# Second norm of a transformer layer: token block 0 normed first, the normed x gathered, gate-up waits by halves, turned h copied first

## The reference

```python
x = layer_norm(DN_ALPHA * x + mixed, ln1_g[l], ln1_b[l])
x = layer_norm(DN_ALPHA * x + memory_cross_attention(x, mem, w_cq[l], w_ckv[l], w_co[l]), ln2_g[l], ln2_b[l])
x = layer_norm(DN_ALPHA * x + moe_ffn(x, w_router[l], router_bias[l], w_exp_gu[l],
                                      w_exp_down[l], w_sh_gu[l], w_sh_down[l]), ln3_g[l], ln3_b[l])
...
scores = jax.nn.sigmoid(jnp.dot(t, w_router).astype(jnp.float32))
choice = scores + router_bias.astype(jnp.float32)
...
gates = jnp.zeros((n_tok, N_EXPERTS), jnp.float32).at[jnp.arange(n_tok)[:, None], idx].set(w).astype(t.dtype)
y = (jax.nn.silu(gu[:, :SHARED_FF]) * gu[:, SHARED_FF:]) @ w_sh_down
for e in range(N_EXPERTS):
    gu = t @ w_exp_gu[e]
    h = jax.nn.silu(gu[:, :EXPERT_FF]) * gu[:, EXPERT_FF:]
    y = y + gates[:, e:e + 1] * (h @ w_exp_down[e])
```

## Time and profile before

| | us |
|---|---|
| median of three runs | 1021.77 (1020.12 to 1022.16) |
| the profiled execution | 1021.97 |
| its span | 1019.80 |
| TensorE busy | 993.3 (97%) |
| VectorE busy | 524.5 (51%) |
| ACT busy | 376.4 (37%) |
| GpSimd busy | 56.3 (6%) |

### The profile page before, as it was taken

How to read it: one execution, slowest core, us unless ns; L and a number is a source line. 1 busy time by engine, 2 the same in 40 slices (tenths; PEclk the granted TensorE clock), 3 DMA queues, 4 the chain that set the end, 5 groups by cost and what they waited for, 6 DMA issues and landing times.

```text
span 1019.8 us, 15454 instructions
## 1 busy us (share of the span) xinstructions
PE 993.3 (97%) x6370; PEld 711.6 (70%) x6371; DVE 524.5 (51%) x1049; ACT 376.4 (37%) x687; POOL 56.3 (6%) x53
## 2 busy tenths in 40 slices
PE   8999999999999999999999999999999999999994
PEld 7998999999999999998974444444444444444432
DVE  6899455675769966855677222322223222222223
ACT  5665435556577744455321211121112111211112
POOL 0000202324200000000010000000000000000000
PEclk9999999999999999999999999999999999999998
DMA  8564534333344555658837999999999999999972
GB/s 305 188 226 146 185 123 167 124 125 125 125 166 166 181 192 182 233 207 350 347 141 280 419 419 421 420 419 420 420 418 420 420 420 420 421 420 419 420 326 83
DMA packets 41653, 290.85 MB, mean 285 GB/s; under 512 B 4712, under 2 KB 5872, under 8 KB 6896
## 3 DMA queue, kind: packets, MB, share of 16 engines
q1 hardware_dynamic: 40800, 284.62, 70.6%
q0 software_dynamic: 784, 5.24, 1.3%
HBM read 288.78 MB, written 1.06 MB: 284 GB/s over the span
## 4 chain that ended last, share of the span: by engine, by line
PE 86%; DVE 10%; issue 2%; DMA 1%; ACT 1%; SPq 0%; ACTq 0%; DVEq 0%
PE stream L1548 24%; PE stream L1876 22%; PE stream L1900 11%; PE stream L1573 8%; PE work L1865 6%; DVE w_lo L972 3%; DVE acc L1008 3%; PE stream L1824 2%; PE stream L1828 1%; PE stream L1826 1%; PE stream L1830 1%; DMA raw<-in_wdense 1%; PE work L1675 1%; PE work L1651 1%; PE work L1851 1%
## 5 line engine op out<-in xcount | busy, mean ns | idle before, releaser
L972 DVE TENSOR_TENSOR w_lo<-raw,w_hi 128x1024 fp32r<-128x1024 f32 x142 | 171.4, 1227 | 57.1 <-ACT w_hi L668 57.0
L1876 PE MATMUL stream<-ring,xg 128*64 128x512 f32 x640 | 197.0, 592 | 0.8 <-issue 0.8
L668 ACT ACTIVATE w_hi<-raw 128x1024 fp32r<-128x1024 f32 x142 | 147.1, 1052 | 53.2 <-DMA raw<-in_wdense 36.4
L1548 PE MATMUL stream<-xT_hi,w_hi 128*128 128x256 f32 x560 | 161.3, 288 | 1.4 <-DVE w_lo L972 1.4
L1548 PE MATMUL stream<-xT_lo,w_hi 128*128 128x256 f32 x560 | 158.6, 283 | 0.0
L1548 PE MATMUL stream<-xT_hi,w_lo 128*128 128x256 f32 x560 | 158.4, 283 | 0.0
L1876 PEld LDWEIGHTS stream<-ring,xg 128*64 128x64 f32 x640 | 63.0, 137 | 91.5 <-issue 90.4
L1548 PEld LDWEIGHTS stream<-xT_hi,w_hi 128*128 128x128 f32 x560 | 106.8, 191 | 6.1 <-issue 3.3
L1548 PEld LDWEIGHTS stream<-xT_lo,w_hi 128*128 128x128 f32 x560 | 106.5, 190 | 0.3 <-issue 0.2
L1548 PEld LDWEIGHTS stream<-xT_hi,w_lo 128*128 128x128 f32 x560 | 106.6, 190 | 0.0
L1425 DVE TENSOR_TENSOR hh<-h,stream 128x256 f32<-128x256 f32 x32 | 13.5, 421 | 172.3 <-ACT h L901 172.3
(11 more groups left out here) (381 smaller groups left out, 2038.1 us busy)
## 6 DMA issues: line engine op xcount, KB each, us to landing
ring<-in_wstream SPq DMA_DIRECT2D x120, 1024.0 KB, 16.1
raw<-in_wdense SPq DMA_DIRECT2D x73, 1024.0 KB, 4.9
place_e<-in_wstream SPq DMA_DIRECT2D x24, 1024.0 KB, 17.1
place_m<-in_wstream SPq DMA_DIRECT2D x12, 1024.0 KB, 14.8
place_c<-in_wstream SPq DMA_DIRECT2D x12, 1024.0 KB, 16.4
place_w<-in_wstream SPq DMA_DIRECT2D x12, 1024.0 KB, 16.0
place_x<-in_wstream SPq DMA_DIRECT2D x12, 1024.0 KB, 17.6
ln<-in_lnp POOLq DMA_DIRECT2D x3, 1024.0 KB, 7.1
```

The lines of the kernel that those rows point to most:

```text
L668: nc.scalar.activation(w_hi[:, q % ROUNDED, :], raw[:, q % 6, :], ACT.Copy).then_inc(w_rounded, 1)
L972: tt(w_lo[:, q % 6, :], raw[:, q % 6, :], w_hi[:, q % ROUNDED, :].bitcast(F32), ALU.subtract).then_inc(w_rest, 1)
L1548: last = mm(S[n % 4][:, 0:SEQ], w[:, b, :], a[:, kb, :], start=(kb + j == 0), stop=(kb == chunks * KB - 1 and j == len(parts) - 1))
L1876: last = mm(S[2][e * SLOTS:(e + 1) * SLOTS, :], feature_block(buf, kb)[:, col + e * SLOTS:col + (e + 1) * SLOTS], tiles[e][kb // 4][:, kb ...
```

## The change

Token block 0 is finished first and turned inside the last co block, token block 1 inside the first sh block; `keep_warm` goes there. The router works per token block, half of the contraction in each of two bands (the bands are added by a matmul with `two_ident`), the sigmoid comes after the scores are turned back. What is gathered is the normed x without gain and bias (`xn_hi`, `xn_lo`); gain and bias are applied when a gathered block leaves PSUM, from a copy of the two tables (`gain2`). `xres` gets them on VectorE later, for the residual, which is now one operation per bank.

SP: half 1 of tile 6 lies where `xres` is and waits for the residual, behind pair 0's gate-up refills:

```diff
-            sp.wait_ge(split_l, 2)
-            expert_halves(6, 6)
+            expert_half(6, 6, 0)
...
+                if pair == 0:
+                    sp.wait_ge(residual_done, 4)
+                    expert_half(6, 6, 1)
```

```diff
-            nc.gpsimd.tensor_tensor(xres[:, 1, :], xres[:, 1, :], ln2[:, 0, :], ALU.mult).then_inc(norm_pool, 1)
-            pool.wait_ge(norm_pool, 1)
-            nc.gpsimd.tensor_tensor(xres[:, 1, :], xres[:, 1, :], ln2[:, 1, :], ALU.add).then_inc(norm_pool, 1)
-            pool.wait_ge(norm_pool, 2)
-            pool.wait_ge(ln_done, TB + 1)
+            pool.wait_ge(proj_ready, DONE[-1])
```

ACT:

```diff
-            act.wait_ge(router_mm, 1)
-            nc.scalar.activation(scoresT[0:EXPERTS, :], W[0][0:EXPERTS, 0:SEQ], ACT.Sigmoid).then_inc(score_sig, 1)
...
+            act.wait_ge(router_mm, 2)
+            nc.scalar.activation(scoresT[:], W[0][:, 0:SEQ], ACT.Copy).then_inc(score_sig, 1)
+            act.wait_ge(router_mm, 3)
+            nc.scalar.activation(scores[:], W[3][:, 0:TB * EXPERTS].rearrange("p (t e) -> p t e", t=TB), ACT.Sigmoid
+                                 ).then_inc(score_sig, 1)
...
+            def leave_gathered(buf, kb, bank):
+                nc.scalar.activation(feature_block(buf, kb), bank[:], ACT.Identity, scale=gain2[:, kb:kb + 1],
+                                     bias=gain2[:, KB + kb:KB + kb + 1]).then_inc(gath_act, 1)
...
-                if pair < LAST_GROUP:
-                    act.wait_ge(gath_mm, KB + 2 * pair + 1)
-                    nc.scalar.activation(feature_block((pair // 4 + 1) % 2, 2 * (pair % 4)), S[1][:], ACT.Copy
-                                         ).then_inc(gath_act, 1)
                 act.wait_ge(hT_mm, pair + 1)
                 nc.scalar.activation(hT[:], S[2][:, 0:2 * P].rearrange("p (k s) -> p k s", k=2), ACT.Copy
                                      ).then_inc(hT_cp, 1)
+                if pair < LAST_GROUP:
+                    act.wait_ge(gath_mm, KB + 2 * pair + 1)
+                    leave_gathered((pair // 4 + 1) % 2, 2 * (pair % 4), S[1])
```

VectorE (its first shared product now comes right after the selection, the second after the one-hot blocks, the gates behind that; the zeros and both rests of x ahead of the scores; gain and bias of `xres` after the first group's slots):

```diff
+            add_output("co", {6: lambda: normalise(1, 0).then_inc(xhat_done, 1), 7: lambda: leave_x2T(0)})
...
-            for t in range(TB):
-                link(tt(geq[:, t], geq[:, t], lower8, ALU.mult))
+            link(tt(geq[:], geq[:], lower8.unsqueeze(1).to_broadcast([P, TB, EGROUPS, EGROUPS]), ALU.mult))
             link(tt(gcmp[:], gcmp[:], geq[:], ALU.add))
             link(nc.vector.tensor_reduce(goff[:], gcmp[:], AX.X, ALU.add))
-            link(ts(gmask[:], goff[:], TOP_GROUPS - 0.5, None, ALU.is_lt))
-            link(ts(goff[:], gmask[:], -MASKED, MASKED, ALU.mult, ALU.add))
-            for t in range(TB):
-                by_group = masked[:, t].rearrange("p (g e) -> p g e", g=EGROUPS)
-                link(tt(by_group, choice[:, t].rearrange("p (g e) -> p g e", g=EGROUPS),
-                        gmask[:, t].unsqueeze(2).to_broadcast([P, EGROUPS, 8]), ALU.mult))
-                link(tt(by_group, by_group, goff[:, t].unsqueeze(2).to_broadcast([P, EGROUPS, 8]), ALU.add))
+            link(ts(gmask[:], goff[:], TOP_GROUPS - 0.5, 0.5, ALU.is_lt, ALU.subtract))
+            link(stt(masked[:].rearrange("p t (g e) -> p t g e", g=EGROUPS),
+                     gmask[:].unsqueeze(3).to_broadcast([P, TB, EGROUPS, 8]), -4.0 * MASKED,
+                     choice[:].rearrange("p t (g e) -> p t g e", g=EGROUPS), ALU.mult, ALU.min))
...
-                            link(stt(bank, x2h[:, t, cols].bitcast(F32), ALPHA, bank, ALU.mult, ALU.add))
-                            stt(bank, x2l[:, t, cols].bitcast(F32), ALPHA, bank, ALU.mult, ALU.add
-                                ).then_inc(residual_done, 1)
+                            stt(bank, xres[:, t, cols], ALPHA, bank, ALU.mult, ALU.add).then_inc(residual_done, 1)
...
+                if pair == 1:
+                    list_items()
```

TensorE:

```diff
+ORDER = {"co": [(0, 0), (1, 0), (0, 1), (1, 1), (0, 2), (0, 3), (1, 2), (1, 3)],
+         "sh": [(0, 0), (0, 1), (1, 0), (1, 1)]}
...
-                if t == 0:
-                    chunk_here(q)
-                    chunk_here(q + 1)
                 for kb in range(KB):
-                    if kb == 4 and midway is not None:
-                        midway()
+                    if kb in midway:
+                        midway[kb]()
+                    if t == 0 and kb % 4 == 0:
+                        chunk_here(q + kb // 4)
...
-                keep_warm(S[0][:, 0:SEQ], ocT_r[0][:, 0, 0:P], ocT_r[0][:, 1, :], 13)
...
+            def scores_of(t):
+                pe.wait_ge(x2T_act, 4 * t + 4)
+                pe.wait_ge(x2T_dve, 4 * t + 4)
+                for step in range(4):
+                    for band in range(2):
+                        kb = 4 * band + step
+                        last = mm(W[0][band * EXPERTS:(band + 1) * EXPERTS, t * P:(t + 1) * P], w_router[:, kb, :],
+                                  x2T[:, kb, t * P:(t + 1) * P], start=(step == 0), stop=(step == 3))
+                last.then_inc(router_mm, 1)
...
+            for k in range(8):
+                token_major("co", k, ocT_r, ready=(cav_rest, 2) if k == 0 else None,
+                            midway={1: lambda: turn_normed(0)} if k == 7 else {})
+            scores_of(0)
+            token_major("sh", 0, x2T, midway={6: lambda: turn_normed(1)})
+            token_major("sh", 1, x2T, midway={3: lambda: scores_of(1), 6: turn_scores})
             token_major("sh", 2, x2T)
...
+            token_major("sh", 3, x2T, midway={4: count_selected})
...
-                if kb < 2:
-                    turn_shared(kb)
-                    pe.wait_ge(sh_silu, kb + 1)
+                if kb in (0, 2):
+                    turn_shared(kb // 2)
...
-                if pair % 4 == 0:
-                    pe.wait_ge(gath_act, 4 + pair)
-                    pe.wait_ge(gath_dve, 4 + pair)
                 def landed(half):
+                    if pair % 4 == 0:
+                        pe.wait_ge(gath_act, 2 + pair + 2 * half)
+                        pe.wait_ge(gath_dve, 2 + pair + 2 * half)
```

More of the change, by code:

```diff
@@ L83, with block_of, last_output @@
 OUT_KIND = [k for k, m, _ in STREAM for _ in range(m)]
+ORDER = {"co": [(0, 0), (1, 0), (0, 1), (1, 1), (0, 2), (0, 3), (1, 2), (1, 3)],
+         "sh": [(0, 0), (0, 1), (1, 0), (1, 1)]}
+def block_of(kind, k):
+    return ORDER[kind][k] if kind in ORDER else (k % TB, k // TB)
+def last_output(kind, m, pair):
+    return max(k for k in range(m) if block_of(kind, k)[1] == pair)
 OUT0, CHUNK0, DONE = {}, {}, []
@@ L828, in _, with norm_sqrt @@
                 round_chunks(out_index("mix", k))
[L829 to L832 removed]
+            def norm_sqrt(which, t):
+                act.wait_ge(ln_var, TB * which + t + 1)
+                nc.scalar.activation(rstd[:, t:t + 1], rvar[:, t:t + 1], ACT.Sqrt).then_inc(ln_sqrt, 1)
             def turned(dst, t):
@@ L866, in _, with round_x @@
                 round_chunks(out_index("co", k))
-            norm_sqrt(1)
+            def round_x(t):
+                act.wait_ge(xhat_done, t + 1)
+                nc.scalar.activation(xn_hi[:, t, :], xres[:, t, :], ACT.Copy).then_inc(split_h, 1)
             for t in range(TB):
+                norm_sqrt(1, t)
+                if t == 0:
+                    round_x(0)
                 act.wait_ge(xt_mm, 4 + 2 * t + 1)
@@ L1780, in _, with turn_normed @@
                 last.then_inc(cav_mm, 1)
-            for k in range(8):
-                token_major("co", k, ocT_r, ready=(cav_rest, 2) if k == 0 else None)
-            bank_free(out_index("sh", 0))
-            for t in range(TB):
+            def turn_normed(t):
                 pe.wait_ge(xhat_done, t + 1)
                 turn(t)
-                keep_warm(S[0][:, 0:SEQ], ocT_r[0][:, 0, 0:P], ocT_r[0][:, 1, :], 13)
-            pe.wait_ge(x2T_act, 8)
-            pe.wait_ge(x2T_dve, 8)
-            for kb in range(KB):
-                last = mm(W[0][0:EXPERTS, 0:SEQ], w_router[:, kb, :], x2T[:, kb, :], start=(kb == 0),
-                          stop=(kb == KB - 1))
-            last.then_inc(router_mm, 1)
+            def scores_of(t):
[7 more added lines that the diff above has]
+                last.then_inc(router_mm, 1)
             def turn_scores():
```

215 lines of the change are left out of this document (105 added, 110 removed).

## The result

| | us |
|---|---|
| before, median of four runs | 1021.93 (1020.12 to 1022.16) |
| changed kernel, median of four runs | 1014.60 (1013.59 to 1015.01) |
| ratio, 95% interval | 0.9933 (0.992 to 0.9947) |
| profiled execution of the changed kernel | 1014.28, span 1012.3 |

The forecast was 1013.1 us in a range of 1010.4 to 1016.6, and faster. The time lies in the range, but the two terms did not come out: the way to pair 0 gave more than was forecast, and the turned h nothing.

What follows compares the result with a forecast made beforehand. The prediction saw a front of chained waits, then a pair loop with TensorE and DMA both nearly full. Profiled 1021.97 - 6.2 (front) - 2.8 (turned h) + 0.1 (gain-table copy) = 1013.1 us, range 1010.4 to 1016.6.

Steps and rivals of the forecast that it cites:

- the way to pair 0: From the last co blocks to pair 0's gate-up: start at 530.4 instead of 536.67, taken as 6.2 us less.
- the turned h: Pair loop, ACT copies h before the gathered block: 0.16 us a pair, 4.5 us, cut to 2.8 by the DMA lead.
- co: Last cross-attention projection blocks: one turning more, 1.09 us, no wait for weights; end at 504.60 instead of 503.51.
- Routers, steps, fold, count: TensorE from 504.60 to the count's end at 521.8: routers 1.1 us each, fold 0.55, count 1.1.
- The table load on the path: ACT's sigmoid table load behind the copy of the scores: 1.28 us, to 514.38, standing on the path.
- the rival of a slower front: Router bands run one after the other and an activation starts 1.4 us later after its table load: 1016.7 us; chance 0.12.
- Selection before the count: Selection done at 520.2, TensorE reaches its count at 520.68, so it no longer waits for the selection.
- Gather phase: Gathered blocks ahead of pair 0: start at 523.9 instead of 528.8, taking 6.5 us instead of 7.85.
- What was costed at nothing: Gain and bias of x (4.9 us if uncovered), item list, shared weights: covered by other work, 0 us.
- the rival that had this case: Something else holds the down projection, so the h move buys nothing: 1015.9 us; chance 0.12.
- The DMA lead: Weight tiles' 5.4 us lead at pair 31: tile 6's second half takes 2.5, 2.9 remain, the loop wants 4.5.
- The clock: Rival: without 26 filler matmuls TensorE's clock falls from 2.4 to 1.2 GHz before pair 0: 1033 us; chance 0.04.

Runs made afterwards that it cites:

- the first kernel whose loop was really shorter: Changed kernel, with VectorE copying the whole turned one-hot block out of its bank first and summing the gates from that copy: 1010.45 us, ratio 0.9894.
- Three variants that opened holes: Changed kernel with natural co order (1019.38 us) or with gain and bias before the gather (1018.86 us); kernel before without its idle matmuls (1023.59 us).
- the four taken away here: Changed kernel with one part undone each: co block order (1019.38 us), router bands (1016.47), gain and bias after gathering (1018.86), gate-up waiting by halves (1016.62).

## Why the prediction was right in size and wrong in its terms

The time came out within the range, and in part by luck: a loop term of 2.8 us that did not come at all was offset by a front 0.5 us better than forecast and by 0.7 us ahead of both, which no term had.

- **co.** Forecast: one turning more, no wait for weights. First to last: 22.77 us before (480.74 to 503.51), 23.87 after, 1.10 more, as the term had it.
- **Routers, steps, fold, count.** Forecast 17.2 us from the end of co to the end of the count, measured 16.70. The turning takes 0.87 and not 1.09, each router 1.02 and not 1.1, the fold 0.39 and not 0.55, the count 0.85 and not 1.1; the 28 steps between them take 12.54 and not 12.24.
- **The table load on the path.** Wrong in place. It ends at 513.51 while TensorE folds until 513.66. The sigmoid starts right behind that:

```profile
512.23 1.28 ACT L894 ACT_TABLE_LOAD   x1
513.70 0.28 ACT L894 ACTIVATE scores<-work 128x128 f32<-128x128 f32 x1 [0.19 <-PE work L1823]
514.00 1.28 ACT L901 ACT_TABLE_LOAD   x1
515.29 0.38 ACT L901 ACTIVATE h<-stream 128x256 f32<-128x256 f32 x1
```

  The last two rows settle one half of the rival of a slower front: the activation starts 1.29 us behind its load's start, nothing is added. The other half, bands one after the other, is settled by the router in one chain (1.89 against 1.02). The Trainium skill ("ScalarE: Activation LUTs", What ACT_TABLE_LOAD costs) adds a drain of about 1380 ns to the 1283 of the load; the load agrees, and the drain is not there in these rows. Nor would it have cost the 1.4 us that the prediction says: in its own schedule the selection is done at 520.2 and the count comes at 520.68, which covers 0.5 of them.
- **Selection before the count.** Right: 519.22 against 519.76, with 0.54 us to spare. The routing took 5.2 us, 5.3 were forecast.
- **Gather phase.** From the end of the count it began 2.28 us later, 2.1 were forecast. 522.89 to 529.22, 6.33 us; 6.5 were forecast. Together the front gave 6.75 us where the sum had 6.2.
- **What was costed at nothing.** Gain and bias, the item list and the shared weights cost nothing that shows: pair 0 to the end takes as long as before. The 0.1 us for the copy of the gain table does not show either.
- **The turned h.** The step that failed: "The matmul itself moves only from 567.41 to where the last gather matmul frees it", 0.16 us a pair. It adds the 0.17 of one view (a piece of the chain, which counts a matmul only until the next one takes over) to the 567.08 of another (the timeline's start). In the timeline's own row that matmul takes 0.34 us, to 567.42, and down starts at 567.41: the matmuls showed no gap to be won. I took the idle time of the weight load for a wait, since one of its sides carried h's name. With h early the hole stayed at 0.25 us (1021.54 us against 1021.58). So the term was worth 0 and not 4.5 us; the rival that had this case stood at 0.12, and its 1015.9 lies as near the measured 1014.6 as the forecast does.

  What makes the hole was not tested; it stands where the form changes from 128*128 to 128*64, and the Trainium skill ("TensorEngine Tiling (Array Packing)", Key Properties) says that changing the tiling mode drains TensorE. The 0.25 us agree with such a drain, and so does the other change of form in each pair, from gate-up to the scatter-add: there TensorE's weight load stands idle for 0.81 us (0.28 between two loads of gate-up itself), and the trace names nothing that it waits for. Neither shows the cause.
- **The DMA lead.** Forecast: tile 6's second half pushes all later tiles back by 2.5 us, or by nothing if it finds the queue empty. It found it empty: the DMA engines had moved nothing since 545.5 when it was issued at 548.6, and it landed at 553.5. The sum took the 2.5 (and its 4.5 less 1.6 of waiting is 2.9, where it has 2.8). The last tile of place_w, in the row that answers to the earlier trace rows:

```profile
L531 SPq DMA_DIRECT2D place_w<-in_wstream x1: 328/328/328, 955.6 to 955.6; - x1
...
DMA to landing us min/median/max: 22.2/22.2/22.2
```

  It landed at 977.8, and its gate-up began at 982.84: 5.0 us are left, where 2.9 were forecast. Before, 5.4 were left, and 6.6 in the variant with h first, whose tile landed 20.7 us behind its issue; so between 0.4 and 1.6 us went, not 2.5, and what took them stays open. The waiting in pair 31 did not come in the changed kernel, since nothing drew on the lead; it came in the first kernel whose loop was really shorter, 1.2 us of it where a gain of 5.9 us met a lead of 5.0.
- **The number.** Forecast for the profiled execution: 6.2 and 2.8 less, 0.1 more. Came: 6.75 less in the front, nothing in the loop, 0.7 less ahead of both, whose cause is open, 0.2 less outside the span (1.98 us instead of 2.17), and no 0.1 more for the copy. A loop term too large by 2.8, against 0.55, 0.70, 0.19 and 0.1 from these and 0.05 from the loop, leaves the 1.2 us between forecast (1013.1) and profiled execution (1014.28).
- **The clock.** The changed kernel kept the full clock, as forecast. Three variants that opened holes show that the risk is real, at a far smaller price: about 1.7 us each, not 20, for the clock was back at 0.9 or more within 4 to 8 us.

## What to carry to other kernels

Before a wait is priced, ask what the engine would do without it: if it has the same idle time when the awaited thing is early, the wait is a name and not a cost. One run with the order swapped showed that here. And take start and length of an instruction from the same view. Where an engine is kept without a hole, the parts of a rebuild can't be valued one by one; two of the four taken away here opened a hole of some 3 us and brought a lower clock behind it. And a step that buys nothing may be what makes another step free, as h ahead of the longer copy: that order saves 0.10 us a pair.

## What the runs showed of the hardware

- Two idle stretches of 1.6 us with 1.1 us of turning between them brought TensorE's granted clock down to 0.67 over the next 4 us. Single holes of 3.08 and 2.93 us gave 0.68 and 0.65. In all three cases the matmuls behind took about 1.7 us longer. Holes of 0.87, 0.50 and 0.83 us within 9 us left it at 1.00.
- Eight fp32 matmuls of 64 output rows and 128 columns took 1.89 us in one chain and 1.02 us in two bands side by side.
- A weight load that follows matmuls of another form stood idle for 0.25 us (128*128 to 128*64, with its operand late or early) and for 0.81 us (128*64 to 128*128). Between gather matmuls of one form it starts with the matmul before it, without idle time.
- The first 140 us of the kernel have more than one course: the v projection began at 139.7 to 140.0 us in eight profiles of the changed kernel and its variants, at 141.3 and 141.4 in two of them, and at 141.0 to 141.2 in the three of the kernel before and its variants. From there to the first co matmul all take 339.7 to 340.5 us, so waiting chunk by chunk shows no gain. Whether the change's one small copy in the first stage has a part in the difference stays open; it is as large as the 0.7 us above.
